# Layer 2's key offsets as bias tables in SBUF instead of passes on the TensorE

## The reference

```
logf = log_sigmoid(f_logit + b_f)                     # one value per frame and head
q_off = cumsum(logf, axis=1)
k_off_past = logf_past - cumsum(logf_past, reverse)   # for the 512 past frames
k_off = concat([k_off_past, q_off])
decay = q_off[query] - k_off[key]
logits = q . k * scale + decay
p = softmax(where(key_pos <= q_pos, logits, -1e30))
o = (p @ v) * sigmoid(g)
```

## Time and profile before

| what | before |
|---|---|
| time, median of 3 runs (lowest to highest) | 1044.56 us (1041.41 to 1046.07) |
| the profiled execution's own time | 1042.3 us |
| its span in the trace | 1040.5 us |
| busy, share of the span: PE, DVE, ACT, POOL | 94%, 42%, 30%, 11% |
| mean granted clock of the TensorE | 0.974 |
| GpSimd busy | 113.6 us in 148 instructions |

### The profile page before, as it was taken

The page is one execution under the profiler, slowest core; times in us unless marked ns, Lnnn a source line. Parts: engine busy times, 40 slices in busy tenths (PEclk is TensorE's granted clock), DMA queues, the critical chain, the costliest instruction groups (busy, mean ns, idle before and its releaser), DMA issues.

```text
span 1040.5 us, 12144 instructions
## 1 busy us (share of the span) xinstructions
PE 974.9 (94%) x4789; PEld 609.8 (59%) x4789; DVE 434.9 (42%) x883; ACT 312.9 (30%) x612; POOL 113.6 (11%) x148
## 2 busy tenths in 40 slices
PE   4999999898999999988989999999798999999997
PEld 3777666686444444433767777776687444444443
DVE  4666467435122312227366525465625122213223
ACT  4544667323111111124244433343313111111110
POOL 5234123200000000001213310100000000000000
PEclk9999989899999999999899999999799999999999
DMA  9735612534999999997233521311555899999991
GB/s 294 267 122 176 196 43 60 196 149 186 368 421 421 421 421 420 357 420 265 81 122 102 192 80 31 107 45 52 204 232 231 328 420 419 421 422 420 420 414 58
DMA packets 53339, 260.30 MB, mean 250 GB/s; under 512 B 5088, under 2 KB 5328, under 8 KB 28704
## 3 DMA queue, kind: packets, MB, share of 16 engines
q1 hardware_dynamic: 47824, 242.64, 59.0%
q0 software_dynamic: 5456, 16.83, 5.4%
HBM read 252.88 MB, written 6.57 MB: 249 GB/s over the span
## 4 chain that ended last, share of the span: by engine, by line
PE 85%; DVE 7%; ACT 3%; DMA 2%; issue 1%; POOL 1%; SPq 0%; DVEq 0%; POOLq 0%
PE ps L1375 21%; PE ps L1391 11%; PE ps L967 7%; PE ps L968 6%; PE ps L969 6%; PE ps L1340 3%; PE ps L1341 2%; PE ps L1404 2%; PE ps L1020 2%; PE ps L1021 2%; PE ps L1196 2%; PE ps L1405 2%; PE ps L1136 2%; PE ps L1192 2%; PE ps L1350 1%; PE ps L1122 1%
## 5 line engine op out<-in xcount | busy, mean ns | idle before, releaser
L1375 PE MATMUL ps<-w_raw,xT 128*64 128x512 f32 x408 | 174.1, 594 | 0.4 <-issue 0.4
L1375 PE MATMUL ps<-w_extra,xT 128*64 128x512 f32 x376 | 131.5, 594 | 4.0 <-DMA w_raw<-in_moe_w_gate 1.3
L1491 DVE TENSOR_TENSOR w_lo<-w_raw,w_hi 128x2048 fp32r<-128x2048 f32 x36 | 82.1, 2288 | 44.6 <-ACT w_hi L670 44.5
L967 PE MATMUL ps<-w_hi,hT_hi 128*128 128x512 f32 x224 | 94.7, 423 | 3.8 <-DVE w_lo L1491 3.1
L1391 PE MATMUL ps<-w_raw,hidT 128*64 128x512 f32 x216 | 96.0, 595 | 0.0
L968 PE MATMUL ps<-w_lo,hT_hi 128*128 128x512 f32 x224 | 90.2, 403 | 0.0
L969 PE MATMUL ps<-w_hi,hT_lo 128*128 128x512 f32 x224 | 90.1, 402 | 0.0
L1375 PEld LDWEIGHTS ps<-w_extra,xT 128*64 128x64 f32 x376 | 40.8, 137 | 82.3 <-issue 82.3
L1375 PE MATMUL ps<-w_more,xT 128*64 128x512 f32 x240 | 88.4, 593 | 0.0
L670 ACT ACTIVATE w_hi<-w_raw 128x2048 fp32r<-128x2048 f32 x36 | 68.4, 1910 | 42.0 <-PE ps L1021 39.3
L1391 PE MATMUL ps<-w_extra,hidT 128*64 128x512 f32 x184 | 71.1, 595 | 0.0
(11 more groups left out here) (290 smaller groups left out, 1771.1 us busy)
## 6 DMA issues: line engine op xcount, KB each, us to landing
w_extra<-in_moe_w_up SPq DMA_DIRECT2D x28, 1024.0 KB, 13.0
w_raw<-in_moe_w_gate SPq DMA_DIRECT2D x27, 1024.0 KB, 10.6
w_raw<-in_moe_w_down SPq DMA_DIRECT2D x27, 1024.0 KB, 11.2
w_raw<-in_moe_w_up SPq DMA_DIRECT2D x24, 1024.0 KB, 12.4
w_extra<-in_moe_w_down SPq DMA_DIRECT2D x23, 1024.0 KB, 13.2
w_extra<-in_moe_w_gate SPq DMA_DIRECT2D x19, 1024.0 KB, 11.7
w_more<-in_moe_w_gate SPq DMA_DIRECT2D x18, 1024.0 KB, 12.8
w_raw<-in_fox_w_in SPq DMA_DIRECT2D x16, 1024.0 KB, 5.4
```

Of the source, the lines that this page charges most:

```text
L967: mm(out, a_hi, b_hi, start=start, stop=False)
L1375: ins = mm(ps[j * CAP:(j + 1) * CAP, bank, :], xT[:, i % 2, kb, j * CAP:(j + 1) * CAP], buffer(U.slot)[:, k * F:(k + 1) * F], start=(kb == ...
L1491: v.tensor_tensor(w_lo[:, U.slot, :], w_raw[:, U.slot, :], w_hi[:, U.hslot, :].bitcast(F32), ALU.subtract).then_inc(lo_ready, 1)
```

## The change

The offsets no longer go through the TensorE. Once the sums are there, the ScalarE copies them into one tile `off` (16 heads by 832 offsets), and GpSimd stores it to a scratch in DRAM. For each pair `load_offsets` reads them back by four DMAs, each of which writes one head's row into all partitions that need it: 256 offsets into 128 partitions (`key_bias`, once for each head), and 576 into 64 partitions (`last_bias`, the same). `add_mask` then waits for all four and adds the causal mask on GpSimd in three instructions; each tells the VectorE that one item's table is ready. `row_max` adds the table where it added the mask. There are two tables of each kind, used in turn, so `load_offsets(p)` waits for the row maxima of pair p-2. The sums are made after block 2 instead of block 1. The flags of the last part (the case in which an expert overflows) share semaphores now; nothing else in that part is new.

```diff
-        pick_heads = sb("pick_heads", [FOX_HEADS, PAIRS, P], F32R)
+        key_bias_1 = sb("key_bias1", [P, 2, 3 * P])
...
-        off_hi = sb("off_hi", [FOX_HEADS, 832], F32R, offset=gain_at)
-        off_lo = sb("off_lo", [FOX_HEADS, 832], F32R, offset=gain_at + 4 * D)
+        off = sb("off", [FOX_HEADS, SEQ + PAST + DEC], offset=gain_at)
+        off_rows = nc.dram_tensor("off_rows", (FOX_HEADS, SEQ + PAST + DEC), F32, kind="Internal").ap()
+        key_bias = [sb("key_bias0", [P, 2, 3 * P], offset=gain_at), key_bias_1]
+        last_bias = [sb(f"last_bias{i}", [P, PAST + DEC], offset=gain_at + 4 * (6 * P + i * (PAST + DEC))) for i in range(2)]
...
+                def load_offsets(p):
+                    if p >= 2:
+
+                        pool.wait_ge(L["max_done"], B["max_done"] + 3 * (p - 2) + 3)
+                    loaded = fox[f"off_loaded{p % 2}"]
+                    for c in range(2):
+                        head = off_rows[2 * p + c, :]
+                        pool.dma_start(key_bias[p % 2][:, c, P:3 * P], head[0:SEQ].partition_broadcast(P)).then_inc(loaded, 16)
+                        pool.dma_start(last_bias[p % 2][c * DEC:(c + 1) * DEC, :], head[SEQ:SEQ + PAST + DEC].partition_broadcast(DEC)).then_inc(loaded, 16)
+
+                def add_mask(p):
+
+                    pool.wait_ge(fox[f"off_loaded{p % 2}"], 64 * (p // 2 + 1))
+                    tile, tri_ = key_bias[p % 2], mask[:, BCOL[0]:BCOL[0] + P].unsqueeze(1).to_broadcast([P, 2, P])
+                    pool.tensor_tensor(tile[:, :, 0:P], tile[:, :, P:2 * P], tri_, ALU.add).then_inc(L["bias_ready"], 1)
+                    pool.tensor_tensor(tile[:, :, 2 * P:3 * P], tile[:, :, 2 * P:3 * P], tri_, ALU.add).then_inc(L["bias_ready"], 1)
+                    last = last_bias[p % 2][:, PAST:PAST + DEC]
+                    pool.tensor_tensor(last, last, mask[:, BCOL[2] + PAST:BCOL[2] + PAST + DEC], ALU.add).then_inc(L["bias_ready"], 1)
...
+                    pool.wait_ge(fox["off_copied"], 2)
+                    pool.dma_start(off_rows, off[:, :]).then_inc(fox["off_stored"], 16)
+                    pool.wait_ge(fox["off_stored"], 16)
+                    load_offsets(0)
+                    load_offsets(1)
                     pool.wait_ge(units_used, IN[l][10].end)
                     pool.dma_start(mask[:, :], A["c_mask"]).then_inc(L["alibi"], 16)
+                    pool.wait_ge(L["alibi"], B["alibi"] + 16)
+                    add_mask(0)
+                    add_mask(1)
...
                 for p in range(2, PAIRS):
                     if p + 2 < PAIRS:
                         load_keys(p + 2)
+                    if l == 1:
+                        load_offsets(p)
+                        add_mask(p)
                     load_values(p)
...
-                    pool.wait_ge(L["scores_done"], B["scores_done"] + 3 * PAIRS)
+                    pool.wait_ge(L["max_done"], B["max_done"] + 3 * PAIRS)
...
-                            if l == 1 and b == 1:
+                            if l == 1 and b == 2:
 
                                 act.wait_ge(fox["off_done"], 1)
-                                A_(off_hi[:, 0:320], ps[0:FOX_HEADS, 7, 0:320], ACT.Copy, scale=-1.0 / SCALE).then_inc(fox["off_hi"], 1)
-                                A_(off_hi[:, 320:832], ps[0:FOX_HEADS, 6, 0:512], ACT.Copy, scale=1.0 / SCALE).then_inc(fox["off_hi"], 1)
+                                A_(off[:, 0:SEQ], ps[0:FOX_HEADS, 7, 0:SEQ], ACT.Copy, scale=-1.0 / SCALE)
+                                A_(off[:, SEQ + PAST:SEQ + PAST + DEC], ps[0:FOX_HEADS, 7, SEQ:SEQ + DEC], ACT.Copy, scale=-1.0 / SCALE).then_inc(fox["off_copied"], 1)
+                                A_(off[:, SEQ:SEQ + PAST], ps[0:FOX_HEADS, 6, 0:PAST], ACT.Copy, scale=1.0 / SCALE).then_inc(fox["off_copied"], 1)
...
-                        elif l == 1:
-                            pe.wait_ge(fox["off_lo"], 2)
+                        if l == 1 and b < 2:
+                            pe.wait_ge(*((fox["f_z"], 1), (fox["off_copied"], 2))[b])
...
-                    if l == 1 and b == 1:
+                    if l == 1 and b == 2:
...
-                def offsets(out, head, n, width, a, stop=True):
-
-                    if width == P:
-                        sel = ident_r[0:FOX_HEADS, head:head + 1].to_broadcast([FOX_HEADS, P])
-                    else:
-                        sel = pick_heads[:, head // 2, :]
-                    mm(out, sel, off_hi[:, a:a + n], start=False, stop=False)
-                    return mm(out, sel, off_lo[:, a:a + n], start=False, stop=True)
-
                 def scores(j, p, t):
                     s = 2 * (j % 2)
                     if j >= 2:
                         pe.wait_ge(L["max_done"], B["max_done"] + j - 1)
-                    fx = l == 1
                     if t < 2:
                         n = KEYS[t]
                         for c in range(2):
 
-                            out = ps[:, s + c, 0:n]
                             cs = slice(c * HD, (c + 1) * HD)
-                            ins = mm(out, qT[cs, p, t * P:(t + 1) * P], kT_new[cs, p, 0:n], start=True, stop=not fx)
-                            if fx:
-                                ins = offsets(out, 2 * p + c, n, P, 0)
+                            ins = mm(ps[:, s + c, 0:n], qT[cs, p, t * P:(t + 1) * P], kT_new[cs, p, 0:n], start=True, stop=True)
                     else:
                         pe.wait_ge(L["past_ev"], B["past_ev"] + p + 1)
-                        ins = mm(ps[:, s, :], q_diag[:, p, :], kT_past[:, p % 2, :], start=True, stop=not fx)
-                        if fx:
-                            offsets(ps[:, s, :], 2 * p, PAST, DEC, 320)
-                        ins = mm(ps[:, s + 1, 0:DEC], q_diag[:, p, :], kT_new[:, p, SEQ:SEQ + DEC], start=True, stop=not fx)
-                        if fx:
-                            ins = offsets(ps[:, s + 1, 0:DEC], 2 * p, DEC, DEC, 256)
+                        ins = mm(ps[:, s, :], q_diag[:, p, :], kT_past[:, p % 2, :], start=True, stop=True)
+                        ins = mm(ps[:, s + 1, 0:DEC], q_diag[:, p, :], kT_new[:, p, SEQ:SEQ + DEC], start=True, stop=True)
...
-                def offsets_lo():
-                    dve.wait_ge(fox["off_hi"], 1)
-                    v.scalar_tensor_tensor(off_lo[:, 0:320], ps[0:FOX_HEADS, 7, 0:320], -1.0 / SCALE, off_hi[:, 0:320].bitcast(F32),
-                                           ALU.mult, ALU.subtract).then_inc(fox["off_lo"], 1)
...
-                        dve.wait_ge(L["alibi"], B["alibi"] + 16)
+                        dve.wait_ge(L["bias_ready"], B["bias_ready"] + 3 * p + t + 1)
...
+                        if l == 0:
+                            add = bias[:, p % 2, a:a + n]
+                        else:
+                            add = last_bias[p % 2][:, :] if t == 2 else key_bias[p % 2][:, c, t * P:t * P + n]
                         ins = v.tensor_tensor_reduce(probs[:, j % 3, c * n:(c + 1) * n], src,
-                                                     bias[:, p % 2, a:a + n] if l == 0 else mask[:, a:a + n], 1.0, -3e38, ALU.add, ALU.max,
+                                                     add, 1.0, -3e38, ALU.add, ALU.max,
```

More of the change, by code:

```diff
@@ L223, in build @@
         b_forget = sb("b_forget", [P, FOX_HEADS])
-        ident_r = sb("ident_r", [P, FOX_HEADS], F32R)
         stat = sb("stat", [P, 160])
@@ L351, in build @@
             sq1=3, rstd1=3, h_ready1=3, tr1=6, ev1=6, h2hi=4, h2lo=3, logits=1, logit_sb=2, gexp=2, selected=1, ranks=2,
-            routed=1, pick_ready=5, gathered=16, slots_act=8, slots_dve=8, slots_tr=16, x_act=8, x_dve=8, pT_done=8, pickT_ready=8, slot_gated=8, silu_done=8,
+            routed=1, flag_ready=1, pick_ready=5, gathered=16, slots_act=8, slots_dve=8, slots_tr=16, x_act=8, x_dve=8, pT_done=8, pickT_ready=8, slot_gated=8, silu_done=8,
             hid_done=8, hT_done=8, hT_copied=8, y0_done=16, y_hi=16, y_lo=16, back_done=24, x_added=24)
@@ L355, in build @@
         BEFORE = [{name: l * n for name, n in per_layer.items()} for l in range(2)]
-        OV = [{name: S(f"{name}{l}") for name in ("flag_ready", "over_load", "over_used", "over_act", "over_hid", "over_tr",
-                                                  "over_ht", "over_done", "over_x")} for l in range(2)]
+        OV = [{name: S(f"{name}{l}") for name in ("over_load", "over_used", "over_act", "over_hid", "over_tr", "over_done", "over_x")} for l in range(2)]
         fox = {name: S(f"fox_{name}") for name in ("wf_loaded", "lp_loaded", "wf_hi", "wf_lo", "f_done", "f_z", "f_exp",
-                                                   "logf_ready", "logf_stored", "heads_ready", "off_done", "off_hi", "off_lo")}
+                                                   "logf_ready", "logf_stored", "off_done", "off_copied", "off_stored", "off_loaded0", "off_loaded1")}
         stores_done = S("stores_done")
@@ L502, in _ @@
                 load_experts(l)
```

(24 more changed lines are left out.)

7 lines of the change are left out of this document (1 added, 6 removed).

## The result

The changed kernel takes 1050.93 us (median of 16 runs, 1045.27 to 1055.86), the kernel before 1042.18 us (median of 16, 1036.65 to 1046.07): a ratio of 1.0086, 95% interval 1.0068 to 1.0105. It is slower, by some 9 us (7 to 11 by the interval). The forecast was 1051, made as 6.2 us on top of the 1044.56 that the kernel before had shown in three runs; the traces' spans are 1040.5 and 1049.1 us.

What follows compares the result with a forecast made beforehand. The TensorE, busy for all 119 us of layer 2's attention, was taken as the bound. Terms -20.6 - 2.5 + 21.8 + 7.5 = +6.2 us on the 1044.56 median gave 1051 us, range 1038 to 1063.

Steps and rivals of the forecast that it cites:

- Removed passes: Layer 2 attention, TensorE: dropping the high and low offset passes saves 2.57 us a pair, 20.6 us in eight.
- Sums moved: Projections: key sums a block later remove the 2.06 us wait and leave 1.4 of the 1.80 one, gaining 2.5 us.
- Table ready: GpSimd's loop, pairs 2 to 5: first table ready 6.5 us after the key load's start, bounds 5.7 and 7.3.
- a sign of being wrong: Attention: copies landing under 2 or over 4.5 us, additions outside 0.3 to 1.0, half-clock stretches absent or 10 us long.
- The waits: Attention, TensorE: late tables cause waits of 6.45, 2.85, 4.1 and 5.4 us in pairs 2 to 5; 21.8 with extras.
- three more of 1.0: Extra 1.0 us waits after gate inversions in pairs 3 and 4, and for inversions and splits of pairs 6 and 7.
- The clock: Attention, TensorE: after the waits, three falls to half clock of 5 us each cost 7.5 us, between nothing and 21.
- The sum: Whole kernel: -20.6 - 2.5 + 21.8 + 7.5 = +6.2 us, giving 1051 us against the median.
- The clock is kept: Rival in the attention: late tables but TensorE keeps its clock, -1.3 us, 1043 us; chance 0.23.
- Faster, the fourth copy lands in 1.7: Rival on GpSimd's copies: quick landing, table ready 4.5 us after the key load, 1035 us, decided near 4.9; chance 0.12.
- Later still, 5 us of landing: Rival on GpSimd's copies: sharing the keys' queue, the fourth lands in 5 us, four clock falls, 1060 us; chance 0.18.
- The rule on ports: Pair 5: by the skill's shared-port rule, GpSimd's second addition would hold up the VectorE's split some 0.6 us at most.

Runs made afterwards that it cites:

- the run without them: The kernel before with the offset passes of the scores left out, all else as it was: ratio 0.9781, 1019.49 us.
- the run with the shorter fills: Changed kernel with 16, 9, 22 and 13 dummy matmuls on the TensorE where it waits for the tables of pairs 2 to 5: ratio 1.0012, 1044.87 us.
- the run of the passes alone: The kernel before with only the offset passes of the scores left out, sums and splits kept: ratio 0.9781, 1019.49 us.
- the run with the copies first: Changed kernel with each pair's table copies and mask additions put ahead of the key load in GpSimd's loop: ratio 0.9757, 1015.18 us.
- the run without reloads: Changed kernel with tables loaded and masked for pairs 0 and 1 only, and reused by pairs 2 to 7: ratio 0.9755, 1019.79 us.

## Why the prediction held

The direction and the mechanism were right: late tables, four waits, half clock. The time was right in part by luck. The forecast difference was 6.2 us and the measured one 8.75; that 1051 meets 1050.93 also comes from the first three runs before, whose median was 2.4 us above that of sixteen. And inside the sum several terms were wrong, with errors that nearly cancel.

**Removed passes**, forecast 20.6: 21.7 by the key loads, 22.8 by the run without them. The starts of neighbouring rows had priced only the passes' own time. The products on either side, which close up once nothing stands between them, give another 1.3 us a pair (3.9 for 2.57), and new waits of some 1.1 us a pair take most of it back.

**Sums moved**, forecast 2.5: 2.0. The wait of 2.06 us went. The second, for which I took 1.4, is now 1.1 us, for the ScalarE's copies, and a gap of 0.48 has come beside it. That the store of the offsets would fit under GpSimd's wait held as well; it took 5.5 us to be back (587.09 to 592.57), not 2.9 + 0.6, and the first table was still done by 604, ahead of the first row maximum at 607.8.

**Table ready**, forecast 6.5 (5.7 to 7.3): 7.0, 7.0, 11.7 and 7.3. In pair 2 the fourth copy lands 3.9 us after its issue (I took 3.3), the addition takes 0.72 (0.6), the issues are a little shorter. Pair 4 is the part that failed: its fourth copy landed 8.6 us after its issue, beyond the 4.5 that I had named as a sign of being wrong. I had priced a landing from rows with next to no other transfer beside them, and did not look what SyncE issues then; its two loads stood in the trace of before too, the first issued at 665.97 us, 3.8 us ahead of pair 4's place in GpSimd's queue.

**The waits**, forecast 6.45, 2.85, 4.1 and 5.4, and three more of 1.0: measured 8.24, 4.63, 10.56, 6.87, so 30.3 in four places for 21.8 in all. Beside the later table, the TensorE arrived 0.4 to 0.9 us sooner than I had it: in pair 2 it begins to wait 4.1 us after the key load (638.10 - 8.24 - 625.74), forecast 5.0. The reason is again the two heads' products: the two score groups became 1.13 + 1.48 = 2.6 us shorter and not 1.58. Of the extra waits the two of pairs 3 and 4 are missing, since the slow clock covered them; they appear in the run with the shorter fills. Those of the last pairs, for which I had 1.0, came: 0.33 and 2.02 us at 714 and 719.5, and 1.36 at 732.5. They stand as well where the tables are early or the old mask is used (0.62, 1.20 and 1.36 in the run of the passes alone), so they belong to the net price of the passes.

**The clock**, forecast three falls of 5 us each, 7.5 us: four falls of 7 to 11 us each, 6 to 8 us net. So the stretches were up to twice as long as I took them (10 us was one of my signs of being wrong), 21.9 busy us at half clock made 11 us, and only since 3 to 5 of these covered other waits does the net sum fit. Nor do the rows bear out a border at a wait of 2.98 us. Waits of 2.06 and 1.80 us left the clock at 1.00, but in the run with the copies first this followed a shorter one:

```profile
666.09 1.08 PE L1208 MATMUL ps<-v_new,dT 128*128 128x64 f32 x8 [1.88 <-DVE o L1675]
...
667.50:670.50 3.00, 3.00 (x9) 1.84 (x8) 0.76 (x4) 1.96 (x6) 0.04 (x1) 0.53 0.53 151
```

And the kernel before has a mean of 0.53 from 615 to 618 us with no wait of the TensorE from 600 us on. Such short stretches stand in some traces and not in others.

**The sum.** -21.7 (passes, net of the new waits) - 2.0 + 28.8 (the four waits less 1.5 that stand in the same places when the tables are early) + 7 = +12.1. Less 1.8 for a half-clock stretch near 615 us that the kernel before has and this one lacks, and less the 1.1 ahead of layer 2, this is +9.2 for a measured 8.6 in the spans. My sum had +6.2: the waits were 7 us too low, the passes 1 us too low, the sums' step 0.5 too high, and the 1.8 and the 1.1 not foreseen at all. The terms are good to a microsecond or so each; that they close to 0.6 us is no proof of any one of them.

**The rivals.** "The clock is kept" falls by the windows. "Faster, the fourth copy lands in 1.7" falls: none landed under 3.3. (Its remark that a table ready 3.6 us after the key load would give the full 23 us was wrong by my own numbers: it would have cleared pair 3, but with its inversion pair 2 needs the table at once.) "Later still, 5 us of landing" was passed in one pair of four (8.6 us), for another reason than the one given. The reading that GpSimd's queue order is the cause, which my forecast had only argued from the order and the rows, is now shown: the same instructions in another order take 34 us less.

**The rule on ports.** In the changed kernel the split of pair 5 took 2.28 us (2.29 before) and the second addition 0.72, so the 0.6 us that I had named did not come there: the split began only once the second addition was done. Where they do meet, in the run with the copies first, the VectorE's row is

```profile
615.67 2.29 DVE L1504 TENSOR_TENSOR w_lo<-w_raw,w_hi 128x2048 fp32r<-128x2048 f32 x1 [1.57 <-ACT w_hi L701]
617.88 0.47 DVE L1675 TENSOR_SCALAR o<-ps,stat 128x64 f32<-128x64 f32 x2
```

and GpSimd's addition, begun at 616.17, lasts until 618.54: 0.58 us past the split's end at 617.96, against its own 0.72. So it waited for the rest of the split, and GpSimd paid. In the changed kernel the VectorE paid once, in pair 7:

```profile
717.70 0.72 POOL L596 TENSOR_TENSOR key_bias<-key_bias,mask 128x256 f32<-128x256 f32 x1 [3.54 <-DMA last_bias<-off_rows]
717.76 1.21 DVE L1699 TENSOR_TENSOR o<-o,gate 64x512 f32<-64x512 f32 x1
718.39 1.17 POOL L597 TENSOR_TENSOR key_bias<-key_bias,mask 128x256 f32<-128x256 f32 x1
```

The gating, begun behind the first addition, took 1.21 us instead of the 0.68 that it takes in the run without reloads, and the second addition, begun behind the gating, 1.17 instead of 0.72. The TensorE's wait for o behind them is 2.02 us against 1.37 in the run without reloads. So the 0.6 us that I had named for pair 5 came, at about that size, in pair 7. By the Trainium skill ("SBUF — State Buffer", section "Who interferes with whom") the one that comes second is blocked until the first is through; the rows agree in all three meetings.

## What to carry to other kernels

When work is taken from the bound engine and given to a queue, look first at what the queue's preceding instruction waits for: four copies behind a load that waited for the transposes turned a gain of 25 us into a loss of 9, and swapping them gave it back. Price a landing under the traffic that will run beside it, from the other queues' issues, and not from a quiet row. A wait on the TensorE can cost more than its length: the four of 4.6 to 10.6 us were each followed by half clock, which added 6 to 8 us to their 30.3. And when passes are taken out from between two matmuls, read the price from a run without them: what stood on either side may close up as well, here by 1.3 us a pair on top of the 2.6 of the passes, and other waits may open.

## What was not expected of the hardware

Two hardware-queue loads of 1 MB raised GpSimd's wait for the last of four small broadcasts (128 and 144 KB each) from 3.4 to 8.1 us; with the copies earlier it was 10.5, beside the same loads, which no run took away there. The products of two heads, 64 rows each, took 0.63 us together when nothing stood between them, as long as those of one head before. A store of 52 KB to DRAM landed 5.2 us after its issue. A GpSimd addition of 256 elements took 0.72 us alone and 2.37 us behind a VectorE instruction with two SBUF inputs. A stretch of some 3 us at half clock followed a TensorE wait of 1.88 us in one run, and none followed waits of 2.06 and 1.80 us in another.
